# VectorE's order at three places of a two-block transformer kernel: rotated latent keys, shared key rows, gate products

## The reference, cut to what matters

```python
def second_block(x, mix_norm_g, w_in, swa_sinks, q_norm_g, w_uq, kv_norm_g, w_ukv,
              w_o_swa, w_o_mla, w_out, ffn_norm_g, w_gate, w_up, w_down, final_norm_g):
        h = rmsnorm_2(x, mix_norm_g[l])
        proj = h @ w_in[l]
        qa, ka, va, q_lat, kv_lat, k_r, g_a, g_b = jnp.split(proj, IN_OFFSETS, axis=-1)
...
        o_a = swa_sink_attention(qa, ka, va, swa_sinks[l])     # 8 heads, window of 128

        cq = rmsnorm_2(q_lat, q_norm_g[l])
        qb = (cq @ w_uq[l]).reshape(B, S, MLA_HEADS, MLA_QK_DIM)
        q_nope, q_rope = jnp.split(qb, [MLA_NOPE_DIM], axis=-1)
        q_rope = apply_rope(q_rope, cos_b, sin_b)
        ckv = rmsnorm_2(kv_lat, kv_norm_g[l])
        kvb = (ckv @ w_ukv[l]).reshape(B, S, MLA_HEADS, MLA_NOPE_DIM + MLA_V_DIM)
        k_nope, vb = jnp.split(kvb, [MLA_NOPE_DIM], axis=-1)
        k_rope = apply_rope(k_r[:, :, None, :], cos_b, sin_b)[:, :, 0, :]
        o_b = mla_attention(q_nope, q_rope, k_nope, k_rope, vb)   # causal, 8 heads

        y = jax.nn.sigmoid(g_a) * (o_a @ w_o_swa[l]) + jax.nn.sigmoid(g_b) * (o_b @ w_o_mla[l])
        x = x + y @ w_out[l]
        h = rmsnorm_2(x, ffn_norm_g[l])
        x = x + (jax.nn.silu(h @ w_gate[l]) * (h @ w_up[l])) @ w_down[l]
```

## Time and profile before

| | us |
|---|---|
| median of 3 runs (1180.85 to 1182.44) | 1182.02 |
| the profiled execution's own time | 1179.61 |
| its span, first to last instruction | 1177.8 |
| PE busy | 1158.9 (98%) |
| DVE busy | 807.0 (69%) |
| ACT busy | 632.7 (54%) |
| POOL busy | 387.2 (33%) |

### The profile page before, as it was taken

The page is one execution under the profiler, slowest core; times in us unless marked ns, Lnnn a source line. Parts: engine busy times, 40 slices in busy tenths (PEclk is TensorE's granted clock), DMA queues, the critical chain, the costliest instruction groups (busy, mean ns, idle before and its releaser), DMA issues.

```text
span 1177.8 us, 17420 instructions
## 1 busy us (share of the span) xinstructions
PE 1158.9 (98%) x6392; PEld 996.0 (85%) x6392; DVE 807.0 (69%) x1667; ACT 632.7 (54%) x1109; POOL 387.2 (33%) x279
## 2 busy tenths in 40 slices
PE   9999999999999999999999999999999999999997
PEld 8888778888888887789878787888889999998886
DVE  5779874775616538599882675682488878787486
ACT  6553574467532355458783787533465545454455
POOL 1418454335554433402463676445500000000000
PEclk9999999999999999999999999999999999999999
DMA  8538874552699584535716611476746666667972
GB/s 269 193 143 242 234 209 175 178 162 108 193 322 216 164 215 117 149 144 133 248 28 126 204 79 36 179 198 158 180 176 191 203 212 191 212 193 257 340 275 95
DMA packets 91093, 216.30 MB, mean 184 GB/s; under 512 B 18425, under 2 KB 28153, under 8 KB 83969
## 3 DMA queue, kind: packets, MB, share of 16 engines
q1 hardware_dynamic: 83232, 180.46, 45.6%
q0 software_dynamic: 4608, 30.41, 12.9%
q10 hardware_dynamic: 3168, 4.33, 1.0%
HBM read 198.24 MB, written 71.45 MB: 229 GB/s over the span
## 4 chain that ended last, share of the span: by engine, by line
PE 84%; DVE 8%; ACT 3%; POOL 2%; issue 1%; SPq 0%; DMA 0%; DVEq 0%; ACTq 0%; POOLq 0%
PE bank L2303 49%; PE bank L2625 15%; PE bank L2639 8%; PE bank L2399 3%; PE bank L2367 3%; PE bank L2381 2%; PE bank L2445 2%; DVE sc L1780 2%; DVE m L1776 1%; POOL w_lo L923 1%; PE bank L2343 1%; PE bank L2484 1%; ACT w_hi L1026 0%; DVE t_lo L2013 0%; DVE mqT L1976 0%
## 5 line engine op out<-in xcount | busy, mean ns | idle before, releaser
L905 POOL TENSOR_TENSOR w_lo<-w_raw,w_hi 128x2048 fp32r<-128x2048 f32 (+4 forms) x48 | 214.2, 4463 | 345.8 <-ACT w_hi L994 289.7
L2303 PE MATMUL bank<-aH,w_hi 128*128 128x512 f32 x544 | 218.7, 402 | 2.6 <-DVE mqT L1976 1.0
L2303 PE MATMUL bank<-aH,w_lo 128*128 128x512 f32 x544 | 212.5, 391 | 0.0
L2303 PE MATMUL bank<-aL,w_hi 128*128 128x512 f32 x544 | 205.8, 391 | 0.0
L994 ACT ACTIVATE w_hi<-w_raw 128x2048 fp32r<-128x2048 f32 (+4 forms) x45 | 83.0, 1844 | 113.9 <-PE bank L2303 93.8
L2625 PE MATMUL bank<-t_hi,w_hi 128*128 128x256 f32 x504 | 142.7, 283 | 0.9 <-DVE fg L1522 0.9
L2625 PE MATMUL bank<-t_hi,w_lo 128*128 128x256 f32 x504 | 142.6, 283 | 0.0
L2625 PE MATMUL bank<-t_lo,w_hi 128*128 128x256 f32 x504 | 142.6, 283 | 0.0
L2013 DVE TENSOR_TENSOR w_lo<-w_raw,w_hi 128x1024 fp32r<-128x1024 f32 (+2 forms) x77 | 106.5, 1392 | 27.9 <-ACT w_hi L1420 21.5
L2303 PEld LDWEIGHTS bank<-aH,w_hi 128*128 128x128 f32 x544 | 102.6, 189 | 22.3 <-issue 4.4
L2303 PEld LDWEIGHTS bank<-aL,w_hi 128*128 128x128 f32 x544 | 102.1, 188 | 22.3
(11 more groups left out here) (414 smaller groups left out, 2638.6 us busy)
## 6 DMA issues: line engine op xcount, KB each, us to landing
w_raw<-in_w_in SPq DMA_DIRECT2D x21, 1024.0 KB, 5.1
w_raw<-up_sums SPq DMA_DIRECT2D x36, 512.0 KB, 4.3
w_raw<-in_gate_up SPq DMA_DIRECT2D x35, 512.0 KB, 4.2
up_sums<-in_gate_up SPq DMA_DIRECT2D x16, 1024.0 KB, 8.7
up_sums<-in_gate_up POOLq DMA_DIRECT2D x8, 1024.0 KB, 10.7
w_raw<-in_w_merge SPq DMA_DIRECT2D x8, 1024.0 KB, 6.2
up_sums<-up_sums POOLq DMA_DIRECT2D x8, 1024.0 KB, 10.9
down_sums<-in_down SPq DMA_DIRECT2D x8, 1024.0 KB, 11.2
```

Source lines behind the costliest of these rows:

```text
L905: pool.tensor_tensor(out=w_lo[:, c % 2, 0:n], in0=w_raw[:, c % 2, 0:n], in1=w_hi[:, c % 2, 0:n].bitcast(F32), op=ALU.subtract).then_inc(w_ ...
L2303: ins = pe.matmul(o, l, r, start=(kk == 0 and operand == ROUNDED and m == 0), stop=(kk == total - 1 and operand == REST), skip_group_check ...
```

## The change: what it does

The diff moves three pieces of VectorE's function; no instruction is added or removed, and no other engine's list changes.

```diff
             for j in range(4):
                 evac("t.sk", j, skS[:, j // 2, j % 2, :])
+            rope_blocks(kvl[:, :, KVR:KVR + MR].rearrange("p b (h d) -> p b h d", h=1), 1, 16, "3", rp2)
             for stage, tiles, hi, lo, g, base in (("t.cq", 3, cqH, cqL, "q", 0), ("t.ck", 2, ckH, ckL, "kv", 3)):
                 for j in range(tiles):
                     dve.wait_ge(c_hi_ready, base + j + 1)
                     empties(dve.scalar_tensor_tensor(
                         out=lo[:, j, :], in0=bank_of(stage, j)[:], scalar=gv[:, GV[g] + j:GV[g] + j + 1],
                         in1=hi[:, j, :].bitcast(F32), op0=ALU.mult, op1=ALU.subtract), stage, j)
-            rope_blocks(kvl[:, :, KVR:KVR + MR].rearrange("p b (h d) -> p b h d", h=1), 1, 16, "3", rp2)
             dve.wait_ge(x_stored, 16)
...
             for q in range(2):
                 low_half(UNITS["ukv"][0], q)
-            for i in range(2):
-                dve.tensor_copy(mK[DH:MQK, i, 0, :], krS[DH:MQK, :]).then_inc(kr_split, 1)
-            dve.wait_ge(kr_split, 2)
-            for i in range(2):
-                dve.tensor_tensor(out=mK[DH:MQK, i, 1, :], in0=krS[DH:MQK, :], in1=mK[DH:MQK, i, 0, :].bitcast(F32),
-                                  op=ALU.subtract).then_inc(kr_split, 1)
             for h in range(H):
                 wait_filled(dve, "t.mq", h // 4)
                 ins = dve.tensor_copy(mqT[DH:MQK, h, :], bank_of("t.mq", h // 4)[MR * (h % 4):MR * (h % 4) + MR, :])
...
                     ins.then_inc(q_roped, 1)
+            for i in range(2):
+                dve.tensor_copy(mK[DH:MQK, i, 0, :], krS[DH:MQK, :]).then_inc(kr_split, 1)
+            dve.wait_ge(kr_split, 2)
+            for i in range(2):
+                dve.tensor_tensor(out=mK[DH:MQK, i, 1, :], in0=krS[DH:MQK, :], in1=mK[DH:MQK, i, 0, :].bitcast(F32),
+                                  op=ALU.subtract).then_inc(kr_split, 1)
             for b in range(NB):
                 splits[0] += 1
...
             first_low(0)
+            gates_out(1, fg, 0)
             block_low(1)
             t_low(3)
             t_low(4)
-            gates_out(1, fg, 0)
             gates_out(1, fu, 2)
```

## The result

| us | before | after |
|---|---|---|
| median (5 runs each) | 1181.09 | 1185.68 |
| lowest to highest | 1180.37 to 1182.44 | 1185.21 to 1188.42 |
| the profiled execution's own time | 1179.61 | 1186.1 |
| its span | 1177.8 | 1184.3 |
| mean granted clock of TensorE | 0.998 | 0.995 |

The ratio after to before is 1.0043, 95% interval 1.0032 to 1.0054: 5.1 us slower (3.8 to 6.4). The three moves together make the kernel slower.

The account below looks back on a forecast made before the run. TensorE was taken to bound the kernel, so only its waits could be won or added to. The terms 0.3 + 4.1 + 2.2 - 1.0 = +5.6 us, on a median of 1182.02, gave 1187.6, range 1182.5 to 1190.5.

Parts of the forecast that it names:

- the likeliest case: Whole kernel: the forecast itself, +5.6 us to 1187.6, with hold-ups by GpSimd and a clock fall; chance 0.50.
- Place A: Rotation moved behind `skS`, ahead of the windowed attention's softmax: first instruction waits for GpSimd, softmax later, +0.3 us.
- Place B: `mK` instructions moved behind `mqT`: they take turns with GpSimd, one instruction each, delaying mla's first maximum, +4.1 us.
- The rival in which subtraction 2 gets in ahead of `w_lo`: Place B: no softmax late, `w_lo` ends about 1.4 later; B +1.4, total +0.7 us; chance 0.13 with a near-equal form.
- The upper bound of +7.6: Place B: the four `mK` instructions get no turn until GpSimd rests at 675.2, +7.6 us; as a rival, chance 0.07.
- Clock at place B: TensorE idle behind `n2`: clock falls to half speed for 4 to 5 us, +2.2 us, bounds 0 and +3.5.
- rival 1: Same terms at the three places, but no fall of TensorE's clock: +3.4 us, 1185.4; chance 0.19.
- Place C: Gate product `fg` moved earlier: TensorE's 0.94 us wait before the first block product goes, -1.0 us.
- the clock at place A: TensorE's wait ahead of the windowed attention: no term, since no idle stretch up to 1.9 us had lowered the clock.
- the 4.1 us form: Place B: GpSimd's long `w_lo` gets its turn ahead of VectorE's subtraction 2, costing 4.1 us.
- the 1.4 us form: Place B: subtraction 2 gets in ahead of GpSimd's long `w_lo`, costing 1.4 us.

Follow-up runs that it names:

- e2_rows: Kernel before with only the four `mK` instructions on the shared key rows moved behind the `mqT` copies: 1188.07 us, ratio 1.0049, +5.8 us.
- e5_rows_busy: As e2_rows, plus 14 useless TensorE matmuls ahead of its wait for `kr_split`: 1185.64 against 1181.15 us for before, ratio 1.0031.
- e4_rows_quarters: As e2_rows, with GpSimd's `w_lo` of `n2`'s second half cut into four instructions: 1182.44 us, ratio 1.0005 to before.
- e1_gates: Kernel before with only the gate product `fg` moved ahead of three low parts: 1179.42 against 1181.16 us, ratio 0.9983.
- e8_best: Kernel before with the edits of e7_rotation_early and e1_gates together: 1178.49 against 1181.15 us, ratio 0.9967.
- e3_rotation: Kernel before with only the six rotation instructions moved to directly behind the `skS` copies: 1181.72 us, ratio 0.9997.
- e7_rotation_early: Kernel before with the six rotation instructions moved ahead of the `skS` copies, behind the reciprocal for `kvl`: 1178.66 us, ratio 0.9976.
- e10_rotation_early_again: The kernel of e7_rotation_early measured once more against before: 1178.54 against 1180.93 us, ratio 0.9979.
- e9_fill_swa: Kernel before plus seven useless TensorE matmuls inside its 1.9 us wait ahead of the windowed attention's unit 2: 1179.77 against 1180.93 us, ratio 0.9993.

## Why the prediction was right

The direction, the likeliest case and nearly all its terms held; one stretch of lost clock was not foreseen. By its steps:

- **Place A, +0.3.** Held: `rp` 3.38 us (3.3 forecast), `cqL` 1.3 late, softmax 0.3 late.
- **Place B, turns.** Held link by link: casts 0.82 and 1.51 us, subtractions 1.67 and 5.04 us (0.8, 1.5, 1.7, about 5). The rival in which subtraction 2 gets in ahead of `w_lo` fell: at 669.36 GpSimd's `mK` ended, VectorE's subtraction 1 ended at 669.91, and GpSimd's `w_lo` went next. The cost was 4.0 us (4.1 forecast) in after, in e2_rows and in e5_rows_busy. e4_rows_quarters shows that this hold-up is the cause. (The upper bound of +7.6 is 7.5 by its own terms.)
- **Clock at place B, +2.2.** The fall came, so rival 1 is out; it cost 2.5 in after, 2.85 in e2_rows, and 2.4 by the medians of e2_rows and e5_rows_busy. The size came out near for a reason that is partly luck, since two errors offset each other: the half clock lasts 6.8 us, not 4 to 5, and it costs not a half of that but 36 to 42%, since TensorE waits for a part of it.
- **Place C, -1.0.** Held: -1.1 at the first block product in after, e1_gates and e8_best, and the second block is not late.
- **The step that failed:** the clock at place A was given no term, on the ground that no idle stretch up to 1.9 us had made it fall. That was true of the one trace at hand and is no rule: behind the same wait the clock fell in the traces of e1_gates, e5_rows_busy and, with the moved rotation, e3_rotation and after, at a cost of 1.5 to 1.6 us each. By the mean clocks at least half of before's executions bear it too, so it enters the difference of the medians only in part; in after two of five executions are at 0.995 (median 1187.3), three at 0.996 (1185.6).

The forecast of 1187.6 stood on a median of 1182.02 from three runs; with five it is 1181.09. Difference against difference it is +5.6 forecast and +5.1 (3.8 to 6.4) measured. The median of 1185.68 by itself would not have told the forecast from rival 1: it lies just below the forecast's own range (1186.0 to 1189.5) and close to rival 1's 1185.4. The difference (rival 1 has +3.4) and the clock in the traces decide between them.

On the lock itself the Trainium skill ("SBUF — State Buffer", section "Who interferes with whom") says that such instructions of VectorE and GpSimd exclude each other for the whole instruction; the 5.04 us subtraction and the 3.38 us `rp` agree. It does not speak of two instructions that are both queued, as the prediction says, but it does say that whoever issues first gets the shared ports. Read so, it speaks for the 4.1 us form and leaves less room to the 1.4 us form than the prediction gave it. The trace agrees: `w_lo` could follow `mK` from 669.36, subtraction 2 could follow subtraction 1 only from 669.91, and `w_lo` went first. The 1.4 us form did not occur.

## What to carry to other kernels

Ahead of moving a VectorE instruction whose inputs are all in SBUF, look at what GpSimd runs at its new time: beside a GpSimd instruction over SBUF it takes as long as that one, and of a string of n, each waits for one of GpSimd's. Such instructions belong into a gap of GpSimd (e7_rotation_early) or beside short ones (e4_rows_quarters), and instructions on PSUM belong beside its long ones. Removing a wait of TensorE of 1.7 to 1.9 us, as at place A, can be worth more than its length, because the clock may fall behind it in some executions. One profile cannot tell this; the times and mean clocks of all executions can, if the half clock at the kernel's end is taken out of the account.

## What the runs showed of the hardware that was not expected

- TensorE's clock falls behind a wait of 1.7 to 1.9 us in some executions and not in others of the same kernel: of the traces with a wait of that length at place A, those of before, e2_rows and e4_rows_quarters show 1.00 there, those of after, e1_gates, e3_rotation and e5_rows_busy 0.50 for 3.4 us. With 0.8 us of wait (e7_rotation_early, e10_rotation_early_again, e8_best) or 0.3 (e9_fill_swa) the clock fell there in none of the four traces.
- The half clock lasted 3.4 us at place A (577.6 to 581.0 in after, 578.95 to 582.37 in e3_rotation, 577.95 to 581.37 in e5_rows_busy) and 6.8 us at place B (676.6 to 683.4 in after, 676.9 to 683.7 in e2_rows), behind the 3.4 us wait that a second one of 0.65 and 0.78 us follows.
- The fall did not set in with the wait: in after TensorE had worked again from 675.74 when the clock fell at about 676.6.
- Matmuls of no use cost nothing inside these waits: 14 in 3.33 us (e5_rows_busy) and 7 in 1.76 us (e9_fill_swa), with the next useful one at the old time.
